# Gated delta rule in a two-block transformer kernel: the convolution's first tap on ScalarE, the decay's column as a bias of the exponential, k times beta in one operation

## The chip, the cores and the metric

The kernel runs on one core of a Trainium2 chip, in one launch. The metric is the device time of that core in microseconds (us), the median of three runs. Matrix products run on TensorE (PE in the profile), elementwise work on VectorE (DVE) and ScalarE (ACT), and GpSimd (POOL) makes the low halves of the weights. SyncE (SP) issues the loads.

## The reference, cut to what matters

512 tokens of width 1024 pass through two layers of a first block and then through a second block. The change is in the second block's gated delta rule: 8 heads, key and value width 128, chunks of 64 tokens.

```python
qkv = jax.nn.silu(_causal_dwconv(jnp.concatenate([qa, ka, va], axis=-1), conv_w[l]))   # 4 taps
...
q = _l2norm(...) * (A_DK ** -0.5); k = _l2norm(...)
beta = jax.nn.sigmoid(beta)
g = -jnp.exp(a_log) * jax.nn.softplus(alpha + dt_bias)
G = jnp.cumsum(g over a chunk)
diff = G[..., :, None] - G[..., None, :]
decay = jnp.where(incl, jnp.exp(jnp.where(incl, diff, 0.0)), 0.0)
L = jnp.where(strict, beta[..., :, None] * kk * decay, 0.0)
rhs = jnp.concatenate([beta[..., None] * v, (beta * jnp.exp(G))[..., None] * k], axis=-1)
sol = triangular_solve(I + L, rhs)
p_intra = einsum("bhncd,bhnjd->bhncj", q, k) * decay
# then a scan over the 8 chunks with q * exp(G), k * exp(g_last - G), exp(g_last)
```

Every projection around it (q, k, v, the output gates, the band attention, the memory attention, the feed-forward) is a dense product with fp32 accuracy.

## The kernel before, in words

**Dense products.** A weight unit is 128x2048 values. ScalarE copies it rounded to its high half (line 2183, `WH<-WR`), GpSimd subtracts to make the low half in pieces of 256 columns (line 3028, `WL<-WR,WH`), and TensorE takes three products for each of 8 slices of the contraction (line 1886: high by high, low by high, high by low). Two buffers hold the halves, so ScalarE's copy of a unit waits until TensorE has finished the unit two before it.

**Order of the work.** A planner (`order`, lines 542 to 1812) writes one list of steps. Each engine's program is that list with the steps that concern the engine, so every engine works in list order and a wait holds all that stands behind it on the same engine. The planner runs a small clock for each engine with estimated costs (the table `ROUGH`, lines 326 to 351; a pair such as `("V", 0.7, 0)` is 0.7 us of VectorE). `weave` (line 504) lets several lanes advance, always the one that is earliest by this clock. The list therefore changes when costs in the table change.

**The delta rule's stage** (`deltanet`, lines 1088 to 1498). Its lanes are the dense projections (`products`), the convolutions, the preparation of each head, the inversion of pairs of heads, the scan over chunks, and the gates. Steps that the change touches:

- `dq1` (line 2775): VectorE multiplies a projected tile of q, k or v by the rows' norm into one of two padded buffers (`pad`). 24 times, 8 heads by 3. A buffer is free again after the last tap, and a projection waits in the planner while both are taken.
- `dq2` (lines 2776 to 2786): the four taps on VectorE. Tap 3 is a `tensor_scalar` (line 2783) with a wait for `dq1` and for the old contents of the destination; taps 2, 1, 0 are multiply-and-add (line 2786). `dq3` (line 2316) is SiLU on ScalarE.
- `gates4` (line 2308): ScalarE copies the turned gate rows to `RC`, four groups of eight columns per block of 128 tokens: G, beta, exp(G), beta's companion for the last decay. Group 0 (G) is read by `p4` alone.
- `p4` (lines 2787 to 2795): G's row, spread by TensorE over a bank, less G's column from `RC` (line 2793), plus a mask into `DT` (line 2795). Then one exponential over 128x512 on ScalarE (line 2331, `pdec`).
- `p4n`, `p4d`, `p12`, `p14` (lines 2796 to 2844): VectorE makes beta over the norm of k, multiplies the decay by it, and multiplies two products by the decay. Step `j1` of the inversion (lines 2853 to 2865) follows `p12`, and each level of the inversion is a round trip between TensorE (lines 2026, 2036, 2045, 2056) and VectorE or ScalarE (lines 2869 to 2877, 2358).
- `p9` (lines 2827 to 2833 and 2340 to 2347): VectorE scales k by a column in four operations of 128x128, then ScalarE scales k by another column in four (`KD`).

Of the kernel before, what the change touches and what calls it, by code (L numbers as in the profile page):

```python
# [94 lines left out]
def memory(nc, ctx):  # L95
# [156 lines left out]
    "nt": ("V:nt",), "dq1": ("V:dq1",), "dq2": ("V:dq2",), "dq3": ("A:dq3",),  # L252
    "p1": ("A:p1q",), "p2": ("A:pks",), "peq": ("V:peq",), "prow": (), "p4": ("V:p4a", "V:p4", "A:pdec"), "p4n": ("V:pkn",), "p4d": ("V:pdn",),
# [22 lines left out]
    "conv_v": "dq1 dq2 padz", "prepare_a": "p1q pks pdec pbv pkd", "prepare_v": "peq pkn psq p4a p4 pdn pbk pum ppt pqd pel",  # L276
# [43 lines left out]
def by_dma(unit):  # L320
# [221 lines left out]
def order(m):  # L542
# [545 lines left out]
    def deltanet(fo, res_toks):  # L1088
# [94 lines left out]
        def convolutions():  # L1183

            for h in range(8):
                for j in range(3):
                    while (h, j) not in pad_of:
                        yield
                    yield from until((read[j], h - 2))
                    pd = pad_of[h, j]  # L1190
                    for k in (3, 2, 1, 0):
                        step("dq2", h, j, k, pad=pd.i, tok=at("dq1", h, j), c_after=cfree["qkv"[j] + str(h % 2)])
                        if k == 0:
                            pd.free(at("dq2", h, j, 0))
                        yield
                    step("dq3", h, j)
                    curved[j].add(h)
                    yield
# [650 lines left out]
def v4(ap):  # L1849
    return ap.rearrange("p (b q) -> p b q", q=P)  # L1850
# [317 lines left out]
def scalar_program(nc, m, o, sems):  # L2168
# [7 lines left out]
    for kind, key, w in o.steps:  # L2176
# [129 lines left out]
        elif kind == "gates4":  # L2306
            ae.wait_ge(*w["tile"].done)
            a.activation(m.RC[:], PB[w["tile"].b][:].rearrange("p (b q r) -> p b q r", b=4, q=4)[:, :, :, 0:8], ACT.Copy).then_inc(sems["rct"], 1)
        elif kind == "gates5":
            ae.wait_ge(*at("rg"))  # L2310
            a.activation(m.RHL[0:32, :], m.R[0:32, :], ACT.Copy)
            a.activation(m.RHL[64:96, :], m.R[64:96, :], ACT.Copy).then_inc(sems["rhi"], 1)
        elif kind == "dq3":
# [15 lines left out]
        elif kind == "p4":  # L2329
            ae.wait_ge(*at("p4", *key))  # L2330
            a.activation(m.DT[:], m.DT[:], ACT.Exp).then_inc(sems["pdec"], 1)
# [122 lines left out]
def vector_program(nc, m, o, sems):  # L2454
# [39 lines left out]
    for kind, key, w in o.steps:  # L2494
# [281 lines left out]
        elif kind == "dq2":  # L2776
# [3 lines left out]
            if k == 3:  # L2780
                ve.wait_ge(*at("dq1", h, j))
                ve.all(w["c_after"])
                v.tensor_scalar(c[:], pad[:, 3:3 + S], tap, None, ALU.mult).then_inc(sems["dq2"], 1)
            else:
                ve.wait_ge(*at("dq2", h, j, k + 1))
                v.scalar_tensor_tensor(c[:], pad[:, k:k + S], tap, c[:], ALU.mult, ALU.add).then_inc(sems["dq2"], 1)
        elif kind == "p4":
            h, = key
            ve.wait_ge(*w["tile"].done)
            ve.wait_ge(*at("rct"))  # L2790
            ve.all(w["after"])
            bank = PB[w["tile"].b]
            v.tensor_tensor(v4(bank[:]), v4(bank[:]), m.RC[:, :, 0, h:h + 1].broadcast_to([P, 4, P]), ALU.subtract).then_inc(sems["p4a"], 1)
            ve.wait_ge(*at("p4a", h))
            v.tensor_tensor(v4(m.DT[:]), v4(bank[:]), over_blocks(m.CON[:, C_INCL:C_INCL + P]), ALU.add).then_inc(sems["p4"], 1)
        elif kind == "p4n":
            h, = key
            x, y = roots_in(PB[w["tile"].b], 4)
            ve.wait_ge(*at("p4", h))
            ve.wait_ge(*at("pks", h))  # L2800
# [26 lines left out]
        elif kind == "p9":  # L2827
# [3 lines left out]
            for i in range(4):  # L2831
                ins = v.tensor_scalar(blk(m.bk[h % 2], i), blk(PB[w["tile"].b], i), m.RC[:, i, 2, h:h + 1], None, ALU.mult)
            ins.then_inc(sems["pbk"], 1)
# [388 lines left out]
```

## Time and profile before

| | |
|---|---|
| median of 3 runs | 2474.83 us |
| lowest and highest run | 2470.92 and 2479.09 us |
| the profiled execution | 2473.95 us |
| its span, first to last instruction | 2472.3 us |
| instructions | 35533 |
| TensorE busy | 98% of the span |
| weight loads busy | 81% |
| VectorE, ScalarE, GpSimd busy | 41%, 38%, 48% |
| mean granted TensorE clock | 0.993 of full speed |

A busy TensorE is not TensorE at its peak, since matmuls overlap and their ends are modelled. A missing fraction of busy time is time in which nothing at all ran on it. The delta rule's stage lies between 1150 and 1560 us of the span.

### The profile page before, as it was taken

What the parts mean: (1) busy time and instruction counts of PE and PEld (TensorE: products, weight loads), DVE (VectorE), ACT (ScalarE), POOL (GpSimd) and SP (SyncE); (2) the same over time, 40 slices, a digit from 0 to 9 for tenths busy, and PEclk for the clock granted to TensorE, in tenths of its full rate; (3) what the DMA queues carried; (4) which work ended last, traced back from release to release, by engine and by line L of the source; (5) the groups of instructions that cost most, each with busy time, mean ns of one, the idle gap of its engine ahead of it and who ended that gap; (6) DMA issues with size and microseconds to landing.
All of it is one profiled execution on the core that took longest, in us unless ns stands there. A gap on an engine that the chain in (4) does not pass through costs nothing.

```text
span 2472.3 us, 35533 instructions
## 1 busy us (share of the span) xinstructions
PE 2425.7 (98%) x14295; PEld 2004.9 (81%) x14295; DVE 1007.0 (41%) x2261; ACT 935.4 (38%) x1435; POOL 1182.7 (48%) x1566
## 2 busy tenths in 40 slices
PE   8999999999999999999999999999999999999998
PEld 6888888888788888888888888877868887888887
DVE  7974211124874211123867774224345333211113
ACT  5553222224563322224544453235553344322221
POOL 5125655654115565655533233443326645655563
PEclk9999999999999999999999999999999999999999
DMA  5532223224632223224211111232213322223222
GB/s 177 139 103 86 102 88 109 99 77 130 164 103 86 103 81 115 85 85 141 94 58 53 53 52 53 81 133 86 69 58 128 116 96 79 96 86 110 103 80 83
DMA packets 42403, 237.17 MB, mean 96 GB/s; under 512 B 4736, under 2 KB 7936, under 8 KB 19712
## 3 DMA queue, kind: packets, MB, share of 16 engines
q1 hardware_dynamic: 39936, 218.13, 25.0%
q0 software_dynamic: 2304, 16.78, 3.3%
q8 instruction: 113, 1.85, 0.3%
q14 instruction: 50, 0.41, 0.1%
HBM read 213.92 MB, written 4.19 MB: 88 GB/s over the span
## 4 chain that ended last, share of the span: by engine, by line
PE 91%; DVE 4%; POOL 2%; issue 1%; ACT 1%; DMA 1%; SPq 0%; DVEq 0%; POOLq 0%; ACTq 0%
PE PB L1886 75%; PE PB L1888 4%; POOL WL L3028 1%; PE PB L1898 1%; PE PB L1923 1%; PE PB L2136 1%; PE PB L2117 1%; DVE cc L2614 1%; PE PB L1970 1%; PE PB L1987 1%; PE PB L2124 1%; DMA WR<-in_w_in 1%; PE PB L2148 1%; PE PB L2164 1%; PE PB L2087 0%
## 5 line engine op out<-in xcount | busy, mean ns | idle before, releaser
L3028 POOL TENSOR_TENSOR WL<-WR,WH 128x256 fp32r<-128x256 f32 (+1 forms) x1444 | 1055.0, 767 | 753.6 <-ACT WH L2183 753.6
L1886 PE MATMUL PB<-HH,WH 128*128 128x512 f32 x1992 | 795.0, 399 | 11.0 <-ACT HH L2198 10.5
L1886 PE MATMUL PB<-HL,WH 128*128 128x512 f32 x1992 | 779.4, 391 | 0.9 <-DVE HL L2506 0.9
L1886 PE MATMUL PB<-HH,WL 128*128 128x512 f32 x1992 | 516.5, 396 | 0.8 <-DMA WL<-WR 0.8
L2183 ACT ACTIVATE WH<-WR 128x2048 fp32r<-128x2048 f32 (+1 forms) x209 | 371.9, 1779 | 245.9 <-PE PB L1886 238.2
L1886 PEld LDWEIGHTS PB<-HH,WH 128*128 128x128 f32 x1992 | 375.8, 189 | 101.2 <-issue 13.7
L1886 PEld LDWEIGHTS PB<-HL,WH 128*128 128x128 f32 x1992 | 375.8, 189 | 76.9 <-issue 1.7
L1886 PEld LDWEIGHTS PB<-HH,WL 128*128 128x128 f32 x1992 | 366.4, 188 | 75.3 <-issue 2.0
L1886 PE MATMUL PB<-BL,WH 128*128 128x512 f32 (+1 forms) x859 | 331.6, 387 | 0.6 <-DVE BL L2515 0.6
L1886 PE MATMUL PB<-BH,WH 128*128 128x512 f32 (+1 forms) x795 | 307.9, 388 | 1.3 <-ACT BH L2218 1.3
L1886 PE MATMUL PB<-BH,WL 128*128 128x512 f32 (+1 forms) x795 | 195.0, 389 | 1.5 <-POOL WL L3028 1.5
L2521 DVE TENSOR_TENSOR X<-X,PB 128x512 f32<-128x512 f32 x79 | 54.3, 687 | 332.3 <-PE PB L1886 332.3
L1886 PEld LDWEIGHTS PB<-BL,WH 128*128 128x128 f32 x859 | 161.5, 188 | 34.0 <-DVE BL L2515 1.4
L1886 PEld LDWEIGHTS PB<-BH,WH 128*128 128x128 f32 x795 | 149.6, 188 | 32.6 <-ACT BH L2218 2.2
L1886 PEld LDWEIGHTS PB<-BH,WL 128*128 128x128 f32 x795 | 148.3, 189 | 33.1 <-POOL WL L3028 3.0
L3043 POOL TENSOR_TENSOR BL<-ff1c,BH 128x512 fp32r<-128x512 f32 x44 | 56.9, 1294 | 168.0 <-ACT BH L2218 168.0
L2218 ACT ACTIVATE BH<-ff1c 128x512 fp32r<-128x512 f32 x44 | 27.8, 632 | 233.4 <-DVE ff1c L2706 233.4
L2471 DVE TENSOR_TENSOR ff1b<-PB,RSTD 128x512 f32<-128x512 f32 x44 | 30.4, 691 | 196.5 <-PE PB L1886 196.5
L2471 DVE TENSOR_TENSOR ff1a<-PB,RSTD 128x512 f32<-128x512 f32 x44 | 30.4, 692 | 176.8 <-PE PB L1886 168.0
L3033 POOL DMA_DIRECT2D WL<-WR x16 | 14.2, 886 | 170.0 <-ACT WL L2186 170.0
L2614 DVE SCALAR_TENSOR_TENSOR cc<-cp,VECS,cc 128x512 f32<-128x512 f32 x120 | 91.4, 809 | 0.0
L2198 ACT ACTIVATE HH<-X,VECS 128x512 fp32r<-128x512 f32 x48 | 33.3, 717 | 110.4 <-DVE X L2521 110.4
(363 smaller groups left out, 2678.4 us busy)
## 6 DMA issues: line engine op xcount, KB each, us to landing
WR<-in_w_gu SPq DMA_DIRECT2D x66, 1024.0 KB, 4.7
WR<-in_w_dn SPq DMA_DIRECT2D x48, 704.0 KB, 4.0
WR<-in_w_in SPq DMA_DIRECT2D x22, 1024.0 KB, 4.8
WL<-WR POOLq DMA_DIRECT2D x16, 1024.0 KB, 6.9
WR<-in_qkv SPq DMA_DIRECT2D x12, 1024.0 KB, 4.7
WR<-in_w_out SPq DMA_DIRECT2D x8, 1024.0 KB, 4.7
WR<-in_qk SPq DMA_DIRECT2D x8, 1024.0 KB, 4.8
WR<-in_gb SPq DMA_DIRECT2D x4, 1024.0 KB, 4.7
```

Source lines behind the costliest of these rows:

```text
L1886: ins = pe.matmul(out[:, 0:n], wt[:, k * cols + j * P:k * cols + (j + 1) * P], x[:, k, t0:t0 + n], start=first, stop=last)
L1888: ins = pe.matmul(out[:, 0:cols], x[:, k, j * P:(j + 1) * P], wt[:, k * cols:(k + 1) * cols], start=first, stop=last)
L1898: ins = pe.matmul(out[:, j0 + b:j0 + b + 1], blk(src, b), ones[:, 0:1], start=(j0 == 0 and b == 0), stop=(b == nb - 1), skip_group_check=True)
L1923: ins = pe.matmul(blk(PB[t.b], i), blk(left, i), blk(right, i), start=True, stop=True)
L2183: a.activation(m.WH[u % 2][:, 0:n], m.WR[u % 2][:, 0:n], ACT.Copy).then_inc(sems["whi"], 1)
L2198: a.activation(m.HH[:, c, :], m.X[:, c, :], ACT.Copy, scale=w["gain"]).then_inc(sems["hh"], 1)
L2218: a.activation(high[:, w["c"], :], w["src"], ACT.Copy).then_inc(sems["bh"], 1)
L2471: v.tensor_tensor(dst, PB[t.b][:, 0:bank_cols], m.RSTD[:], ALU.mult).then_inc(sems[name], 1)
L2521: v.tensor_tensor(m.X[:, c, :], m.X[:, c, :], PB[w["tile"].b][:], ALU.add).then_inc(sems["res"], 1)
L2614: v.scalar_tensor_tensor(m.cc[j][:], m.cp[j][:, k:k + S], vec(f"dw_w{l}", 2 * k + j), m.cc[j][:], ALU.mult, ALU.add).then_inc(sems["tap"], 1)
L3028: g.tensor_tensor(m.WL[u % 2][:, part], m.WR[u % 2][:, part], f32(m.WH[u % 2][:, part]), ALU.subtract).then_inc(sems["wlo"], 1)
L3043: g.tensor_tensor(m.BL[:, w["c"], :], w["src"], f32(high[:, w["c"], :]), ALU.subtract).then_inc(sems["blg"], 1)
```

## The change

What it does:

1. Tap 3 becomes a step of its own, `dq0`, on ScalarE: an activation Copy with the tap's weight as a column scale. Tap 2 on VectorE waits for it. The wait for the destination's old contents moves from VectorE to ScalarE.
2. `RC`'s group 0 is stored negated, in a copy of its own. The subtraction on VectorE (line 2793) goes; the exponential on ScalarE becomes four of 128x128, each with the block's column of minus G as bias.
3. `p9` on VectorE becomes one operation over 128x512 with the column broadcast.
4. The planner's table follows: `dq0` 0.75 on ScalarE, `dq2` 0.78 to 0.8, `p4` from 1.4 and 2.0 to 0.7 and 1.5 (VectorE and ScalarE), `p9` from 1.7 and 1.6 to 0.7 and 1.1.

```diff
-    "p4": [("V", 1.4, 0), ("A", 2.0, 0)],
+    "p4": [("V", 0.7, 0), ("A", 1.5, 0)],
-    "p9": [("V", 1.7, 0), ("A", 1.6, 0)],
+    "p9": [("V", 0.7, 0), ("A", 1.1, 0)],
+    "dq0": [("A", 0.75, 0)],
...
-                    for k in (3, 2, 1, 0):
-                        step("dq2", h, j, k, pad=pd.i, tok=at("dq1", h, j), c_after=cfree["qkv"[j] + str(h % 2)])
+                    step("dq0", h, j, pad=pd.i, tok=at("dq1", h, j), c_after=cfree["qkv"[j] + str(h % 2)])
+                    yield
+                    for k in (2, 1, 0):
+                        step("dq2", h, j, k, pad=pd.i, tok=at("dq0", h, j))
...
-            a.activation(m.RC[:], PB[w["tile"].b][:].rearrange("p (b q r) -> p b q r", b=4, q=4)[:, :, :, 0:8], ACT.Copy).then_inc(sems["rct"], 1)
+            turned = PB[w["tile"].b][:].rearrange("p (b q r) -> p b q r", b=4, q=4)
+            a.activation(m.RC[:, :, 0, :], turned[:, :, 0, 0:8], ACT.Copy, scale=-1.0)
+            a.activation(m.RC[:, :, 1:4, :], turned[:, :, 1:4, 0:8], ACT.Copy).then_inc(sems["rct"], 1)
...
+        elif kind == "dq0":
+            h, j = key
+            ae.wait_ge(*at("dq1", h, j))
+            ae.all(w["c_after"])
+            a.activation(m.cqkv[h % 2][j][:], m.pad[w["pad"]][:, 3:3 + S], ACT.Copy, scale=vec("conv2", 72 + 8 * j + h)).then_inc(sems["dq0"], 1)
...
             ae.wait_ge(*at("p4", *key))
-            a.activation(m.DT[:], m.DT[:], ACT.Exp).then_inc(sems["pdec"], 1)
+            ae.wait_ge(*at("rct"))
+            for i in range(4):
+                ins = a.activation(blk(m.DT, i), blk(m.DT, i), ACT.Exp, bias=m.RC[:, i, 0, h:h + 1])
+            ins.then_inc(sems["pdec"], 1)
...
-            if k == 3:
-                ve.wait_ge(*at("dq1", h, j))
-                ve.all(w["c_after"])
-                v.tensor_scalar(c[:], pad[:, 3:3 + S], tap, None, ALU.mult).then_inc(sems["dq2"], 1)
-            else:
-                ve.wait_ge(*at("dq2", h, j, k + 1))
-                v.scalar_tensor_tensor(c[:], pad[:, k:k + S], tap, c[:], ALU.mult, ALU.add).then_inc(sems["dq2"], 1)
+            ve.wait_ge(*(at("dq0", h, j) if k == 2 else at("dq2", h, j, k + 1)))
+            v.scalar_tensor_tensor(c[:], pad[:, k:k + S], tap, c[:], ALU.mult, ALU.add).then_inc(sems["dq2"], 1)
...
-            v.tensor_tensor(v4(bank[:]), v4(bank[:]), m.RC[:, :, 0, h:h + 1].broadcast_to([P, 4, P]), ALU.subtract).then_inc(sems["p4a"], 1)
...
-            for i in range(4):
-                ins = v.tensor_scalar(blk(m.bk[h % 2], i), blk(PB[w["tile"].b], i), m.RC[:, i, 2, h:h + 1], None, ALU.mult)
-            ins.then_inc(sems["pbk"], 1)
+            v.tensor_tensor(v4(m.bk[h % 2][:]), v4(PB[w["tile"].b][:]), m.RC[:, :, 2, h:h + 1].broadcast_to([P, 4, P]), ALU.mult).then_inc(sems["pbk"], 1)
```

## Rows read from the trace of the kernel before

**Rows 1.** The profile page, busy time of each engine over the span

```profile
PE 2425.7 (98%) x14295; PEld 2004.9 (81%) x14295; DVE 1007.0 (41%) x2261; ACT 935.4 (38%) x1435; POOL 1182.7 (48%) x1566
```

**Rows 2.** The chain that ended last, by engine, whole span

```profile
PE 91%; DVE 4%; POOL 2%; issue 1%; ACT 1%; DMA 1%; SPq 0%; DVEq 0%; POOLq 0%; ACTq 0%
```

**Rows 3.** Busy time by stretch: the delta rule's stage as one stretch

```profile
core 0: us, PE busy (x) PEld busy (x) DVE busy (x) ACT busy (x) POOL busy (x), PEclk, DMA share, GB/s
...
1150.00:1560.00 410.00, 401.06 (x4337) 340.11 (x4336) 270.86 (x669) 186.45 (x347) 160.62 (x200) 0.99 0.20 70
```

**Rows 4.** Waits of TensorE in the stage: us in total, times, longest

```profile
PE PB L2026 <- DVE TC L2865: 2.2, 2, 1.5
...
PE PB L2045 <- DVE TC L2874: 1.1, 1, 1.1
...
PE PB L2056 <- DVE YC L2877: 0.6, 1, 0.6
PE PB L2104 <- ACT UT L2369: 0.5, 1, 0.5
PE PB L2036 <- DVE YC L2869: 0.5, 1, 0.5
PE PB L1886 <- DVE UM L2471: 0.5, 1, 0.5
```

**Rows 5.** Busy time by stretch, columns as in rows 3: five slices of 20 us

```profile
1250.00:1270.00 20.00, 18.15 (x386) 14.41 (x386) 12.01 (x23) 6.63 (x11) 6.29 (x8) 0.91 0.16 56
...
1310.00:1330.00 20.00, 18.47 (x374) 15.35 (x374) 16.93 (x45) 4.37 (x14) 6.64 (x8) 1.00 0.16 55
...
1390.00:1410.00 20.00, 19.47 (x412) 16.43 (x411) 18.02 (x58) 6.51 (x11) 6.03 (x8) 1.00 0.16 55
1410.00:1430.00 20.00, 17.49 (x327) 15.06 (x326) 13.04 (x22) 8.61 (x17) 7.54 (x8) 0.83 0.06 10
...
1470.00:1490.00 20.00, 19.24 (x352) 16.14 (x351) 16.32 (x54) 7.12 (x13) 6.02 (x8) 1.00 0.15 48
```

**Rows 6.** Groups by line, the stage: the tap on VectorE that moves

```profile
L2783 DVE TENSOR_SCALAR cv<-pad,VECS 128x512 f32<-128x512 f32 x8 | 6.0, 744 | 0.1
...
L2783 DVE TENSOR_SCALAR cq<-pad,VECS 128x512 f32<-128x512 f32 x8 | 4.5, 562 | 0.1
...
L2783 DVE TENSOR_SCALAR ck<-pad,VECS 128x512 f32<-128x512 f32 x8 | 4.4, 549 | 0.0
```

**Rows 7.** Groups by line (first row) and the timeline (second): p4's subtraction, p9

```profile
L2793 DVE TENSOR_TENSOR PB<-PB,RC 128x512 f32<-128x512 f32 x8 | 5.5, 690 | 0.0
...
1402.00 1.12 DVE L2832 TENSOR_SCALAR bk<-PB,RC 128x128 f32<-128x128 f32 x4
```

**Rows 8.** ScalarE with a column operand: groups by line and form, and the timeline

```profile
L2198 ACT ACTIVATE HH<-X,VECS 128x512 fp32r<-128x512 f32 x48 | 33.3, 717 | 110.4 <-DVE X L2521 110.4
...
L2394 ACT ACTIVATE bp<-bp,bsm 128x128 f32<-128x128 f32 x16 | 6.2, 389 | 0.2 <-DVE bsm L2947 0.2
...
1403.16 1.14 ACT L2346 ACTIVATE KD<-PB,SMALL 128x128 f32<-128x128 f32 x4 [5.51 <-DVE bk L2832]
```

**Rows 9.** Timeline: one head's exponential, the table load and the SiLU behind it

```profile
1304.80 0.63 ACT L2331 ACTIVATE DT<-DT 128x512 f32<-128x512 f32 x1 [1.64 <-DVE DT L2795]
...
1305.45 1.28 ACT L2316 ACT_TABLE_LOAD   x1
1306.74 0.63 ACT L2316 ACTIVATE cv<-cv 128x512 f32<-128x512 f32 x1
```

**Rows 10.** Timeline: VectorE standing in order ahead of an inversion

```profile
1308.18 0.69 DVE L2471 TENSOR_TENSOR pad<-PB,RSTD 128x512 f32<-128x512 f32 x1 [2.58 <-PE PB L1886]
```

**Rows 11.** Timeline: ScalarE's queue ahead of an inversion's step, and TensorE behind it

```profile
1499.42 1.90 ACT L2183 ACTIVATE WH<-WR 128x2048 fp32r<-128x2048 f32 x1
...
1502.92 0.38 ACT L2358 ACTIVATE YC<-PB 32x256 f32<-32x256 f32 x1
1503.40 0.69 PE L2056 MATMUL PB<-ZC,YC 32*32 32x32 f32 x32 [0.91 <-issue]
```

More of the change, by code:

```diff
@@ L251 @@
     "gates4": ("A:rct",), "gates5": ("A:rhi", "V:rlo"),
-    "nt": ("V:nt",), "dq1": ("V:dq1",), "dq2": ("V:dq2",), "dq3": ("A:dq3",),
-    "p1": ("A:p1q",), "p2": ("A:pks",), "peq": ("V:peq",), "prow": (), "p4": ("V:p4a", "V:p4", "A:pdec"), "p4n": ("V:pkn",), "p4d": ("V:pdn",),
+    "nt": ("V:nt",), "dq1": ("V:dq1",), "dq0": ("A:dq0",), "dq2": ("V:dq2",), "dq3": ("A:dq3",),
+    "p1": ("A:p1q",), "p2": ("A:pks",), "peq": ("V:peq",), "prow": (), "p4": ("V:p4", "A:pdec"), "p4n": ("V:pkn",), "p4d": ("V:pdn",),
     "p5": (), "p6": ("V:psq",), "p6v": ("A:pbv",),
@@ L275 @@
     "ffn_v": "ff1 ff3 ff", "gates_v": "rcol c1 ab dtb udt dcum rg rlast rlo", "gates_a": "beta edt alog ldt reg rdec rct rhi",
-    "conv_v": "dq1 dq2 padz", "prepare_a": "p1q pks pdec pbv pkd", "prepare_v": "peq pkn psq p4a p4 pdn pbk pum ppt pqd pel",
+    "conv_v": "dq1 dq2 padz", "prepare_a": "p1q pks pdec pbv pkd", "prepare_v": "peq pkn psq p4 pdn pbk pum ppt pqd pel",
     "invert_v": "jz0 jz jt jy kv kz", "invert_a": "jd ka iut iwt", "scan_v": "c0 c1u c4", "zgate_v": "za1 zg1 zg",
@@ L2329, in scalar_program @@
         elif kind == "p4":
+            h, = key
             ae.wait_ge(*at("p4", *key))
-            a.activation(m.DT[:], m.DT[:], ACT.Exp).then_inc(sems["pdec"], 1)
+            ae.wait_ge(*at("rct"))
+            for i in range(4):
+                ins = a.activation(blk(m.DT, i), blk(m.DT, i), ACT.Exp, bias=m.RC[:, i, 0, h:h + 1])
+            ins.then_inc(sems["pdec"], 1)
         elif kind == "p6v":
@@ L2789, in vector_program @@
             ve.wait_ge(*w["tile"].done)
-            ve.wait_ge(*at("rct"))
             ve.all(w["after"])
             bank = PB[w["tile"].b]
-            v.tensor_tensor(v4(bank[:]), v4(bank[:]), m.RC[:, :, 0, h:h + 1].broadcast_to([P, 4, P]), ALU.subtract).then_inc(sems["p4a"], 1)
-            ve.wait_ge(*at("p4a", h))
             v.tensor_tensor(v4(m.DT[:]), v4(bank[:]), over_blocks(m.CON[:, C_INCL:C_INCL + P]), ALU.add).then_inc(sems["p4"], 1)
@@ L2799, in vector_program @@
             ve.wait_ge(*at("p4", h))
+            ve.wait_ge(*at("rct"))
             ve.wait_ge(*at("pks", h))
```

6 rows, old and new, of the table ROUGH are left out of this document.

## The prediction

> **What bounds the kernel now.** The page comes first. TensorE is busy for 2425.7 of 2472.3 us, VectorE for 41% and ScalarE for 38% [rows 1], and the chain that ended last runs through TensorE for 91% and through VectorE for 4% [rows 2]. All that any change to the other engines can win is in the 46.6 us in which TensorE does nothing, and in time at a lowered clock. The next view is the busy time by stretch. In the stage of the delta rule, 410 us long, TensorE is busy for 401.1, VectorE for 270.9 (66%), ScalarE for 186.5 (45%) [rows 3]. So 8.9 us of idle TensorE lie in the stage, and the other 37.7 lie where the change has no instruction.
>
> The third view tells what ended TensorE's waits there. Five rows name VectorE: 2.2 + 1.1 + 0.6 + 0.5 + 0.5 = 4.9 us; one names ScalarE, 0.5 us [rows 4]. The slices show where. In the three in which VectorE is busy for over 16 of 20 us, TensorE loses 1.5, 0.5 and 0.8 us, 2.8 together; two others lose 1.9 and 2.5, at a granted clock of 0.91 and 0.83 of full speed [rows 5]. Those means say that 1.8 and 3.4 us of full-speed work were lost to the lower of the two levels (1.2 GHz in place of 2.4), 5.2 us together. Each dip stands in a slice where TensorE had just gone idle.
>
> **The parts of the change, on the engines.** The moved tap takes 4.5 + 4.4 + 6.0 = 14.9 us of VectorE, 24 operations [rows 6]. The subtraction takes 8 x 0.69 = 5.5 [rows 7]. Scaling k by a column takes 1.12 us a head in four operations; the subtraction that goes has the very form of the new one (a bank, a broadcast column, 128x512) at 0.69, so 8 x 0.43 = 3.4 are saved [rows 7]. VectorE gives up 23.8 us: 270.9 becomes 247.1, 60% of the stage.
>
> ScalarE takes 24 copies of 128x512 with a column as scale, at the 0.72 us of such a copy: 17.3 us. The exponential, 0.63 us in one operation [rows 9], becomes four. No row shows four exponentials from SBUF with a column bias behind each other. From below they cost the 1.14 us of four copies with a column [rows 8], from above four single exponentials of 128x128 with a column, 4 x 0.389 = 1.56 [rows 8]. I take 1.2, since one such exponential is only some 0.02 longer than one such copy. That is 8 x 0.57 = 4.6 us more, between 4.1 and 7.4. The second copy of the gate columns is one small operation, under 0.4 us, once. Together 22 us: ScalarE goes from 186.5 to 208.5, 51% of the stage. Neither engine is full before or after. No DMA is added or moved, and GpSimd and the loads keep their steps.
>
> Two chains have to be looked at besides. For a head's decay they were 0.69 + 0.69 + 0.63 = 2.0 us (subtraction, mask, exponential) and become 0.69 + 1.2 = 1.9. For a tap, 0.62 us (14.9 / 24) on VectorE become 0.72 on ScalarE, and two handovers between engines come in; a handover to an idle engine costs little, to a busy one it costs that engine's queue. The added wait for the gate columns at the exponential is met long before, as the columns are made once at the stage's start.
>
> **The sum on TensorE's path.** First, VectorE's earlier freedom. It can be worth nothing, or all 4.9 us that name it. It is not all: ahead of the 1.5 us lost in the slice from 1310, VectorE itself had stood for 2.58 us waiting for a projected tile of TensorE [rows 10], and time saved before such a wait is only a longer wait. I take the losses in the three slices where VectorE is over 16 of 20 us busy, 2.8, and two thirds of them, as 9% less work brings those slices to about 15 to 16.5: **-2.0 us**. Second, the clock. The dip of 3.4 us lies in a slice where VectorE is busy for only 13 of 20 us, so less work there need not fill the hole: **0**, with -5.2 as the end of the range. Third, ScalarE's queue. At 1499 a weight copy of 1.9 us stands ahead of a piece of the inversion; TensorE idles 0.91 us until that piece is there [rows 11]. With the 0.5 us named above, 1.4 us of TensorE hang on a late ScalarE now. 12% more work on it gives 0.2, and the 24 new handovers push steps of this kind back as well: **+0.5**, between 0 and the rival's price below. Fourth, the planner's list. Its table takes p4's part on ScalarE down from 2.0 to 1.5 us, but table load and exponential took 1.28 + 0.63 = 1.9 [rows 9] and will take 1.28 + 1.2 = 2.5. Where the load does not fall into a wait, VectorE's multiplication of the decay stands 1.0 us longer than planned: up to 8 us over 8 heads, if no other work covers it. In the row, the exponential had waited 1.64 us for VectorE [rows 9], long enough for the load to be hidden: **0**. A rewritten list also moves the dense products between the inversion's steps, with either sign and no row to price it; the stage's 8.9 us of idle time bound the gain.
>
> The sum is -2.0 + 0 + 0.5 + 0 = **-1.5 us**. Against the profiled execution (span 2472.3, 1.65 us around it, 2473.95 in all) that is 2472.4. The profiled one lies 0.9 under the median, so the median should be 2474.8 - 1.5 = **2473.3 us**. A measurement of this kernel can tell about 0.3%, 7.4 us, from no change, and this is within it.
>
> The Trainium skill ("ScalarE: Activation LUTs", What ACT_TABLE_LOAD costs) says that a switch of tables costs the load of about 1.28 us and a drain of about 1.38 besides. The trace does not agree: the load begins 0.02 us after the exponential ends, and the SiLU starts 0.01 after the load [rows 9]. By the page a head's exponential would be due 1.4 us later, and the fourth term's end would be 19 us in place of 8.
>
> **Rival A, VectorE's queue was the bound: faster.** A freer VectorE lets every inversion step answer at once, TensorE has no hole, and the clock does not fall. That gives 4.9 + 5.2 = 10.1 us, 2464.7. For it: the slices with the busiest VectorE lose, and the projections wait for the convolution's buffers in the planner. Against it: [rows 10], and that the deepest slice has a VectorE busy only 65%.
>
> **Rival B, the new handover: slower.** The first tap stands in ScalarE's queue behind a weight copy of 1.9 us [rows 11] or a table load and SiLU of 1.9 [rows 9]. VectorE works in order, so while it stands at the second tap the inversion's steps behind it wait too, and TensorE with them. At 51% busy, the mean rest of what ScalarE is doing, half of 0.8 us or so (208.5 us over some 400 operations, the long ones weighing more), is about 0.4 us. Times 24, if all of it reaches TensorE: 9.6 us, 2484.4. It decides the sign beyond noise from 7.4 / 24 = 0.31 us of TensorE's time for each handover. Against it: the planner knows of the handover and lets other lanes go between, and VectorE has 163 us of idle time in the stage. The Trainium skill has a rule that speaks against this move ("ScalarE: Activation LUTs", Rules for kernel authors): multiplications and additions belong on VectorE, not on ScalarE. The rows bear it out for the single operation, 0.62 against 0.72 us, and leave open whether it matters.
>
> **Rival C, nothing.** Both engines' saved and added time falls into their idle time: 2474.8. Copies with a column have no table load of their own in the stage, so no hidden load spoils it.
>
> **The chances.** The forecast has 0.38 and rival C 0.24; both are within 0.3%, 0.62. Rival A, all cases below 2467.4, has 0.25. Rival B, all above 2482.3, has 0.13. The range from 2463.5 to 2483 leaves out about 0.08 below and 0.10 above.
>
> **What the changed profile would show.** VectorE near 247 us in the stage and ScalarE near 208; the new copy at 0.72; the exponential's blocks at 0.3 to 0.4 each, 1.2 for four; one operation of 0.69 for k. TensorE's idle time in the stage between 6 and 9 us. If rival A is right, rows of TensorE waiting for VectorE vanish and the clock's two dips with them. If B is right, waits of VectorE's second tap for ScalarE stand there with several us, and new holes in the inversions. The prediction is wrong if idle time in the stage changes by more than 7 us, or if the later stages, whose instructions are the same, move by as much because of the new list.

## The result, and the profile after

The changed kernel takes 2493.57 us (median of 6 runs, 2489.97 to 2496.61), the kernel before beside it 2477.16 us (6 runs, 2470.92 to 2479.09). The ratio is 1.0071, 95% interval 1.0059 to 1.0084: 16.4 us slower, beyond the 0.3% that a measurement can tell. The forecast was 2473.3 us, its range ended at 2483.0.

The profiled execution took 2493.78 us. Its page, the busy times (beside [rows 1]) and, further down the page, the chain that ended last (beside [rows 2]):

```profile
PE 2431.7 (98%) x14295; PEld 2006.8 (81%) x14295; DVE 984.1 (39%) x2205; ACT 956.1 (38%) x1484; POOL 1175.5 (47%) x1566
...
PE 91%; DVE 4%; POOL 2%; issue 1%; ACT 1%; DMA 1%; SPq 0%; DVEq 0%; POOLq 0%; ACTq 0%
```

The page hardly differs. VectorE has lost 22.9 us of work, ScalarE gained 20.7, as foreseen, and the chain has the same shares. The loss shows only by stretch. After, the delta rule's stage, the later stages, and three slices of the stage (columns as in [rows 3]):

```profile
1150.00:1580.00 430.00, 407.39 (x4336) 342.29 (x4335) 247.31 (x613) 207.05 (x395) 153.70 (x200) 0.97 0.19 67
1580.00:2492.50 912.50, 890.30 (x4607) 731.60 (x4605) 281.02 (x667) 317.56 (x511) 459.43 (x631) 0.99 0.27 94
1220.00:1240.00 20.00, 12.04 (x176) 9.56 (x175) 12.54 (x23) 10.93 (x24) 7.14 (x8) 0.74 0.28 102
1410.00:1430.00 20.00, 15.60 (x426) 12.09 (x425) 11.91 (x34) 4.14 (x11) 3.50 (x5) 0.74 0.16 55
1490.00:1510.00 20.00, 17.84 (x386) 14.34 (x385) 12.46 (x39) 6.28 (x10) 5.57 (x8) 0.83 0.16 55
```

Before, the later stages:

```profile
1560.00:2472.30 912.30, 889.92 (x4605) 731.65 (x4604) 280.66 (x667) 317.43 (x511) 459.68 (x630) 0.99 0.27 94
```

The later stages take 912.5 us against 912.3. All of the loss, 20 us of the profiled span, lies in the delta rule's stage, which does the same number of matmuls (4336, and 4337 in [rows 3]) in 430 us for 410. TensorE is idle in it for 430 - 407.39 = 22.6 us, against 8.9: 13.7 more. The other 6.3 us are busy time, and the granted clock goes with it: 0.97 over the stage for 0.99. The clock and the holes are in the same slices. In the slices from 1220 and 1410 the granted clock is 0.74, and TensorE is idle for 8.0 and 4.4 us.

What ended TensorE's waits in the stage after (columns as in [rows 4]):

```profile
PE PB L2028 <- DVE TC L2869: 8.0, 1, 8.0
PE PB L2038 <- DVE YC L2873: 4.1, 1, 4.1
PE PB L2058 <- issue: 3.9, 2, 2.0
```

The longest wait of before was 1.5 us [rows 4]. Here one wait alone is 8.0, at the first step of the first inversion. The timeline after, around it:

```profile
1222.49 1.64 PE L1888 MATMUL PB<-HH,WL 128*128 128x512 f32 x6
...
1223.43 1.28 ACT L2343 ACT_TABLE_LOAD   x1
...
1224.72 1.28 ACT L2343 ACTIVATE DT<-DT,RC 128x128 f32<-128x128 f32 x4
...
1226.03 0.69 DVE L2819 TENSOR_TENSOR DT<-DT,PB 128x512 f32<-128x512 f32 x1 [1.67 <-ACT DT L2343]
1226.82 0.69 DVE L2843 TENSOR_TENSOR UM<-PB,DT 128x512 f32<-128x512 f32 x1
1227.54 3.06 DVE L2864 SCALAR_TENSOR_TENSOR ZC<-UM,CON 32x256 f32<-32x256 f32 x4
...
1230.64 0.83 DVE L2867 TENSOR_TENSOR ZC<-ZC,CON 128x256 f32<-128x256 f32 x1
1231.50 0.45 DVE L2869 STREAM_TRANSPOSE TC<-ZC 128x256 f32<-128x256 f32 x1
...
1232.09 1.08 PE L2028 MATMUL PB<-TC,UM 32*32 32x32 f32 x64 [7.96 <-DVE TC L2869]
```

From 1224.13 (1222.49 + 1.64) to 1232.09 ScalarE and VectorE make the inversion's first operand (the decay's exponential, two products, then the operand itself), as they must in either kernel. The point is TensorE's column: behind six dense matmuls (L1888) the very next thing in its program is L2028. Nothing is listed between. Before, the same place is covered. The timeline before, the dense products that go on behind the same six and the inversion's first step:

```profile
1222.52 1.63 PE L1886 MATMUL PB<-HH,WL 128*128 128x512 f32 x6
1223.99 0.39 PE L1886 MATMUL PB<-HH,WH 128*128 128x512 f32 x1
...
1235.63 0.75 PE L2026 MATMUL PB<-TC,UM 32*32 32x32 f32 x64
```

The same 14 us as one stretch (busy time by stretch), before:

```profile
1222.00:1236.00 14.00, 14.00 (x112) 11.65 (x113) 11.55 (x24) 6.33 (x13) 6.00 (x8) 1.00 0.37 125
```

After:

```profile
1222.00:1236.00 14.00, 6.04 (x145) 4.55 (x143) 10.13 (x18) 8.20 (x17) 7.14 (x8) 0.72 0.07 28
```

VectorE is no busier in this stretch than before (10.13 us for 11.55). TensorE has no dense product to do.

Two readings of this fit so far. Either the new instructions make the chain later than the planner thinks (rival B, or the underpriced `p4`), or the list itself is worse, and any instructions would run badly in it. The planner can be asked as well. It prints no time of the chip, but its own clock says when it believes TensorE to be free. Run for the two kernels, it gives for the end of the stage, and for what TensorE stands idle in the plan:

```
          TensorE's clock at the stage's end   idle TensorE in the stage's plan
before    1661.4                               22.4
after     1685.5                               46.5, of it 8.48 ahead of the first inversion's first step
```

The hole of 8 us thus stands in the plan, and could have been read there before anything ran. The planner's clock has no unit that can be trusted (a plan's 24.1 us are 16.4 on the chip), but the hole is in the plan.

### The profile page after: what moved, and what is told of

Same layout as the page of the kernel before. It is cut to its first block, busy times and chain, and to the rows that moved or that the text cites. A ratio compares the mean times of both kernels' runs of the same rounds, so it can differ in the third digit from the quotient of the medians.

```text
span 2492.5 us, 35533 instructions
## 1 busy us (share of the span) xinstructions
PE 2431.7 (98%) x14295; PEld 2006.8 (81%) x14295; DVE 984.1 (39%) x2205; ACT 956.1 (38%) x1484; POOL 1175.5 (47%) x1566
## 4 chain that ended last, share of the span: by engine, by line
PE 91%; DVE 4%; POOL 2%; issue 1%; ACT 1%; DMA 1%; SPq 0%; DVEq 0%; POOLq 0%; ACTq 0%
PE PB L1888 75%; PE PB L1890 4%; POOL WL L3032 1%; PE PB L1925 1%; PE PB L1900 1%; PE PB L2138 1%; PE PB L2119 1%; DVE cc L2627 1%; PE PB L1972 1%; PE PB L2126 1%; PE PB L1989 1%; DMA WR<-in_w_in 1%; PE PB L2150 1%; PE PB L2166 1%; PE PB L2089 1%
## 5 line engine op out<-in xcount | busy, mean ns | idle before, releaser
L1888 PE MATMUL PB<-HH,WH 128*128 128x512 f32 x1992 | 797.4, 400 | 10.3 <-ACT HH L2200 9.8
L1888 PE MATMUL PB<-HL,WH 128*128 128x512 f32 x1992 | 781.2, 392 | 2.0 <-DVE HL L2519 2.0
L1888 PE MATMUL PB<-HH,WL 128*128 128x512 f32 x1992 | 517.0, 396 | 0.9 <-DMA WL<-WR 0.9
L1888 PEld LDWEIGHTS PB<-HH,WH 128*128 128x128 f32 x1992 | 376.6, 189 | 100.9 <-issue 13.7
L1888 PEld LDWEIGHTS PB<-HL,WH 128*128 128x128 f32 x1992 | 376.8, 189 | 78.1 <-DVE HL L2519 2.5
L1888 PEld LDWEIGHTS PB<-HH,WL 128*128 128x128 f32 x1992 | 365.2, 188 | 74.8 <-issue 2.0
L1888 PE MATMUL PB<-BL,WH 128*128 128x512 f32 (+1 forms) x859 | 331.4, 387 | 0.6 <-DVE BL L2528 0.6
L1888 PE MATMUL PB<-BH,WH 128*128 128x512 f32 (+1 forms) x795 | 307.9, 388 | 1.3 <-ACT BH L2220 1.3
L1888 PE MATMUL PB<-BH,WL 128*128 128x512 f32 (+1 forms) x795 | 195.1, 389 | 1.5 <-POOL WL L3032 1.5
L1888 PEld LDWEIGHTS PB<-BL,WH 128*128 128x128 f32 x859 | 161.5, 188 | 34.0 <-DVE BL L2528 1.4
L1888 PEld LDWEIGHTS PB<-BH,WH 128*128 128x128 f32 x795 | 149.5, 188 | 32.6 <-ACT BH L2220 2.2
L1888 PEld LDWEIGHTS PB<-BH,WL 128*128 128x128 f32 x795 | 148.5, 189 | 33.2 <-POOL WL L3032 3.0
```

Source lines behind the costliest of these rows:

```text
L1888: ins = pe.matmul(out[:, 0:n], wt[:, k * cols + j * P:k * cols + (j + 1) * P], x[:, k, t0:t0 + n], start=first, stop=last)
```

## The experiments

### The list against the instructions

Two kernels separate them. `new_ops_old_list` has all of after's instructions, while the planner counts them by the costs of before and counts the tap as VectorE's, so that the list of steps is the one of before, step for step. The entries of the table that change:

```diff
-    "dq0": [("A", 0.75, 0)], "dq2": [("V", 0.8, 0)],
+    "dq0": [("V", 0.78, 0)], "dq2": [("V", 0.78, 0)],
-    "p4": [("V", 0.7, 0), ("A", 1.5, 0)],
+    "p4": [("V", 1.4, 0), ("A", 2.0, 0)],
-    "p9": [("V", 0.7, 0), ("A", 1.1, 0)],
+    "p9": [("V", 1.7, 0), ("A", 1.6, 0)],
```

> All of the change's instructions, but the planner's table keeps the old costs and counts the first tap as 0.78 us of VectorE, so every engine works through the list of before. Theory L (the loss comes from the new list: the planner has both padded buffers held, lists no dense product ahead of an inversion, and TensorE runs dry there): the loss of 16.4 us is gone, the time is 2470 to 2479 us, and TensorE's wait of 8 us near 1232 us is not there. Rival E (the loss comes from the handover to ScalarE's queue, whatever the list): 2488 to 2498 us, with VectorE's second tap waiting for ScalarE and holes in the inversions.

`old_ops_new_list` is the converse: before's instructions (tap on VectorE, subtraction, one exponential, k in four), in the list of after. The tap is a step `dq0` of its own for that, planned as ScalarE's and executed by VectorE. Against before, the entries of the table that change and the step:

```diff
+    "dq0": [("A", 0.75, 0)], "dq2": [("V", 0.8, 0)],
...
+    "p4": [("V", 0.7, 0), ("A", 1.5, 0)],
...
+    "p9": [("V", 0.7, 0), ("A", 1.1, 0)],
...
+        elif kind == "dq0":
+            h, j = key
+            ve.wait_ge(*at("dq1", h, j))
+            ve.all(w["c_after"])
+            v.tensor_scalar(m.cqkv[h % 2][j][:], m.pad[w["pad"]][:, 3:3 + S], vec("conv2", 72 + 8 * j + h), None, ALU.mult).then_inc(sems["dq0"], 1)
```

> The instructions of before (first tap on VectorE, subtraction on VectorE, one exponential, four operations for k), in the list that the changed table gives. Theory L: slow like the changed kernel or slower, 2490 to 2500 us, with TensorE waiting about 8 us before the first inversion. Rival E: as before, 2472 to 2480 us.

Measured: the new instructions in the old list 2479.35 us beside 2477.92, ratio 1.0005 (0.9995 to 1.0015, 11 runs). The old instructions in the new list 2495.07, ratio 1.0069 (1.0056 to 1.0081, 5 runs). After itself is 1.0071. So the instructions, all of them together, are worth nothing that can be measured in either list, and the list is worth the whole loss. The longest waits of TensorE in `old_ops_new_list`:

```profile
PE PB L2028 <- DVE TC L2867: 7.4, 3, 6.7
PE PB L2038 <- DVE YC L2871: 4.2, 1, 4.2
```

Its timeline at the same place:

```profile
1223.50 1.64 PE L1888 MATMUL PB<-HH,WL 128*128 128x512 f32 x6
1231.84 1.08 PE L2028 MATMUL PB<-TC,UM 32*32 32x32 f32 x64 [6.70 <-DVE TC L2867]
```

The same hole at the same place, 6.70 us long for 7.96, without one changed instruction. The new instructions lengthen this one by 1.3 us and the total by nothing.

The stage of `new_ops_old_list` by stretch:

```profile
1150.00:1560.00 410.00, 399.76 (x4325) 338.93 (x4324) 249.79 (x613) 206.73 (x395) 155.22 (x195) 0.98 0.20 70
```

Its timeline at the same place, TensorE:

```profile
1223.56 1.64 PE L1888 MATMUL PB<-HH,WL 128*128 128x512 f32 x6
1225.04 0.39 PE L1888 MATMUL PB<-HH,WH 128*128 128x512 f32 x1
```

Dense products follow the six again, and TensorE idles for 10.2 us of the stage's 410, for 8.9 before. The five waits that the prediction's first term was built on ([rows 4], 4.9 us, all naming VectorE) are still there, each with the total that it had, although VectorE now has 249.8 us of work in the stage in place of 270.9. Waits of TensorE in `new_ops_old_list`:

```profile
PE PB L2028 <- DVE TC L2869: 2.2, 3, 1.5
...
PE PB L2047 <- DVE TC L2878: 1.1, 1, 1.1
...
PE PB L2058 <- DVE YC L2881: 0.6, 1, 0.6
...
PE PB L2038 <- DVE YC L2873: 0.5, 1, 0.5
PE PB L1888 <- DVE UM L2484: 0.5, 1, 0.5
```

This run decides on rival B too. Its mechanism was VectorE standing at the second tap. Waits of VectorE in `new_ops_old_list`, then in after:

```profile
DVE cv L2794 <- ACT cv L2321: 9.7, 2, 7.1
DVE cq L2794 <- ACT cq L2321: 5.8, 3, 3.2
```

```profile
DVE cv L2794 <- ACT cv L2321: 3.2, 3, 1.3
DVE cq L2794 <- ACT cq L2321: 1.0, 1, 1.0
```

VectorE stands 15.5 us at the handover where the kernel loses nothing that can be measured, and 4.2 us where it loses 16. So the handover does not make the loss. What it costs by itself no run shows apart from what the freed VectorE gives: the two together come to +1.2 us, between -1.2 and +3.7 by the interval of the ratio.

### Which part makes the list worse

`tap_only` has the moved tap and its costs, the decay and `p9` as before. `decay_only` has the decay's bias and k in one operation with their costs, the tap on VectorE.

The table of `tap_only`, against after (its instructions for the decay and for k are before's too):

```diff
-    "p4": [("V", 0.7, 0), ("A", 1.5, 0)],
+    "p4": [("V", 1.4, 0), ("A", 2.0, 0)],
...
-    "p9": [("V", 0.7, 0), ("A", 1.1, 0)],
+    "p9": [("V", 1.7, 0), ("A", 1.6, 0)],
```

The lane in `decay_only`, against after (the tap's cost and instruction are before's again too):

```diff
-                    step("dq0", h, j, pad=pd.i, tok=at("dq1", h, j), c_after=cfree["qkv"[j] + str(h % 2)])
-                    yield
-                    for k in (2, 1, 0):
-                        step("dq2", h, j, k, pad=pd.i, tok=at("dq0", h, j))
+                    for k in (3, 2, 1, 0):
+                        step("dq2", h, j, k, pad=pd.i, tok=at("dq1", h, j), c_after=cfree["qkv"[j] + str(h % 2)])
```

> Only the first tap moves to ScalarE, with its costs in the table; the decay and k times beta stay as before. The planner's own clock has the delta rule's stage end 46.9 us later than for the kernel before (24.1 us later for the whole change). Theory L, with the tap's handover as its cause: clearly slower than before, 2495 to 2530 us, slower than the whole change. Rival E: about the whole change's loss, 2485 to 2497 us. A third reading (the decay's and k's cheaper costs spoil the list, not the tap): as before, 2472 to 2480 us.

> The decay's column as a bias and k times beta in one operation, with their costs in the table; the first tap stays on VectorE. The planner's own clock has the stage end 3.1 us earlier than before. Theory L: 2468 to 2477 us, as before or up to 6 us faster. Rival E: as before too, 2472 to 2480 us, since the tap's handover is not there. The third reading (these costs spoil the list): 2488 to 2498 us.

Measured: `tap_only` 2514.75 us, ratio 1.0142 (1.0128 to 1.0155, 4 runs). `decay_only` 2477.44, ratio 1.0001 (0.9989 to 1.0013, 11 runs). The tap alone loses twice what the whole change loses, and the decay's part alone is worth nothing. The parts do not add (1.42% and 0.01% for a whole of 0.71%). On top of the moved tap, the lower costs of `p4` and `p9` give half of the loss back (1.0142 to 1.0071); alone they give nothing. `tap_only`'s waits of TensorE, of the kind seen after:

```profile
PE PB L2028 <- DVE TC L2867: 14.8, 3, 7.3
PE PB L2038 <- DVE YC L2871: 4.5, 2, 3.0
```

### Why the tap does it: the convolutions' lane

In the planner the convolutions are one lane. For each of 24 tiles it issues `dq1`, the taps and the SiLU, and each step moves the lane's own time to where that step can start. With the tap on ScalarE the lane waits twice a tile for ScalarE's place in the plan, once for the tap and once for the SiLU, and the next tile's taps queue behind both. The dates of the planner for the first head that matters say so (end of `dq1`, of the first tap, of the last tap, of the SiLU), and the last SiLU of the stage:

```
                 before                             after
head 1, q        1209.6 1225.3 1233.0 1234.1        1209.7 1226.6 1234.4 1237.8
head 1, k        1228.3 1238.9 1242.4 1243.5        1227.5 1241.7 1244.6 1245.7
head 1, v        1238.1 1244.3 1246.6 1249.0        1235.1 1250.7 1260.0 1261.1
last SiLU        1515.4                             1542.3
```

While both padded buffers are held, the lane of the dense projections waits in the planner. The plan of after says that this is so at the hole. In the 8.48 us without TensorE the two buffers hold head 1's v and head 2's q. The projection behind them is computed and stands at the wait for a free buffer, and the last tap that frees one (head 1's v, 1260.0 in the plan, 1246.6 before) is listed behind the inversion's first step. Of TensorE's idle time in the stage's plan, the part in which the dense lane stands at that wait is 12.5 of 22.4 us before, 29.6 of 46.5 after, and 46.4 of 69.4 in `tap_only`.

Two kernels try the cause. The diffs leave out unchanged lines (marked by dots) and the name of the new lane in the call of `weave`. `tap_own_lane` is after with the same instructions and costs, but the tap is issued from a lane of its own, so that a tile's tap can be placed while the tile before it is still in its taps:

```diff
-                    while (h, j) not in pad_of:
+                    while (h, j) not in begun:
...
-                    yield from until((read[j], h - 2))
...
-                    step("dq0", h, j, pad=pd.i, tok=at("dq1", h, j), c_after=cfree["qkv"[j] + str(h % 2)])
-                    yield
...
+        def first_taps():
...
+            for h in range(8):
+                for j in range(3):
+                    while (h, j) not in pad_of:
+                        yield
+                    yield from until((read[j], h - 2))
+                    step("dq0", h, j, pad=pad_of[h, j].i, tok=at("dq1", h, j), c_after=cfree["qkv"[j] + str(h % 2)])
+                    begun.add((h, j))
+                    yield
```

> The changed kernel, but in the planner the first tap is a lane of its own instead of the first step of the convolutions' lane: it may be listed as soon as its tile is in a padded buffer, while the tile before it still waits for its SiLU. Instructions and table are those of the changed kernel. Theory S (the loss comes from the convolutions' lane being serial: with the tap on ScalarE each tile waits twice for ScalarE's place in the plan, 24 tiles come later, and TensorE has nothing to list between the inversions' steps): 2470 to 2482 us; the planner's own clock has the stage end at 1659.4, 1685.5 for the changed kernel and 1661.4 for the one before. Theory B (the cause is the number of padded buffers alone, which stay held longer whatever the lanes): 2486 to 2498 us.

`three_pads` leaves the lanes alone and gives the convolutions a third padded buffer:

```diff
-    m.pad = (pad0, pad1)
+    pad2, = run(spot["bv1"] + 2048, spot["z0"], ("pad2", [P, 3 + S]))
+    m.pad = (pad0, pad1, pad2)
...
-        pads = Ring([Room(0), Room(1)], clock)
+        pads = Ring([Room(0), Room(1), Room(2)], clock)
```

> The changed kernel with a third padded buffer for the convolutions. Theory B (TensorE runs dry because both padded buffers are held): 2472 to 2482 us. Theory S (the serial lane sets the pace; a buffer more only moves the holes): the hole of 8 us ahead of the first inversion goes, others take its place, 2488 to 2500 us (the planner's own clock: 1685.7, as for the changed kernel).

Measured: `tap_own_lane` 2471.32 us beside 2476.8, ratio 0.9978 (0.9969 to 0.9987, 12 runs). The loss is gone and a little is gained. `three_pads` 2499.99, ratio 1.0092 (1.0076 to 1.0108, 4 runs): no cure. The stage of `tap_own_lane` by stretch:

```profile
1150.00:1560.00 410.00, 404.51 (x4338) 342.19 (x4337) 247.24 (x614) 208.14 (x396) 156.66 (x199) 0.98 0.20 71
```

VectorE's and ScalarE's work is that of after to within 1.1 us. TensorE's idle time is 5.5 us in 410, for 22.6 in 430.

Longest waits in `three_pads`:

```profile
PE PB L2029 <- DVE TC L2870: 9.2, 3, 3.3
PE PB L2081 <- DVE SS L2915: 6.6, 2, 3.6
PE PB L2039 <- DVE YC L2874: 6.0, 2, 3.0
```

The hole of 8 us is broken up (no wait is over 3.6 us), but others take its place, at other inversions and in the scan. So the place of the tap in a serial lane is shown to be the cause: moving that one step to another lane, with every instruction and cost kept, takes the loss away. A third buffer did not help, and the planner's idle TensorE stayed at 46.7 (46.5 after, 20.5 with the own lane). The plan says why. In eight of the ten longest holes of `three_pads` all three buffers are held, and the dense lane stands at its wait for one in 24.2 us of the 46.7, against 5.3 with the tap's own lane. Full buffers are how the dense products are kept out. That they are full comes from the slow lane that empties them, and one more is soon full too.

### The other ScalarE step in the lane

If a serial lane is the trouble, the SiLU in it is a second wait for ScalarE, in before too. Three kernels move `dq3` to a lane of its own: `after_silu_lane`, `decay_silu_lane` (from `decay_only`) and `before_silu_lane`.

```diff
-                    step("dq3", h, j)
+                    tapped.add((h, j))
...
+        def silus():
...
+            for h in range(8):
+                for j in range(3):
+                    while (h, j) not in tapped:
+                        yield
+                    step("dq3", h, j, tok=at("dq2", h, j, 0))
```

> The changed kernel, but the SiLU behind the taps gets a lane of its own in the planner, so that the convolutions' lane waits for ScalarE's place once per tile, as in the kernel before, though now for the first tap. Theory S: 2466 to 2480 us (planner's own clock 1657.7). If the tap's own wait is what costs, whatever else is in the lane: 2486 to 2498 us.

> The first tap stays on VectorE; the decay's bias and k times beta in one operation are in; the SiLU gets a lane of its own, so that the convolutions' lane never waits for ScalarE's place. Planner's own clock: 1648.5, 12.9 us before that of the kernel before. Theory S: faster than both kernels, 2462 to 2472 us. If the planner's clock says nothing about small gains: 2472 to 2480 us.

> The kernel before with nothing but the SiLU in a lane of its own in the planner. It tells whether the gain of the run with the SiLU's own lane belongs to the lane or to the lane together with the change. Planner's own clock: 1668.0 for the end of the stage, 1661.4 for the kernel before. If the lane alone gains: 2464 to 2472 us. If it gains only with the change's cheaper VectorE work (as the planner's clock has it): 2476 to 2488 us.

Measured: `after_silu_lane` 2467.56 us, ratio 0.9955 (0.9940 to 0.9971, 6 runs). `decay_silu_lane` 2471.06, ratio 0.9975 (0.9962 to 0.9988, 12 runs). `before_silu_lane` 2482.97 beside 2477.11, ratio 1.0028 (1.0017 to 1.0040, 6 runs). The same edit wins 1.2% on after (1.0071 to 0.9955), 0.3% on `decay_only`, and loses 0.3% on before. The first of the three says more on the cause. The tap's step is still in the lane there, and the loss is gone all the same. So it takes both waits for ScalarE in one lane, the tap's and the SiLU's, and taking out either is enough. The rule "a lane of its own is better" is wrong as a rule, though the last two differences are no larger than the 0.3% that a measurement can tell; what the lane is worth depends on the costs in the table beside it.

One question was whether the new instructions are at last worth something in this better list. `old_ops_silu_list` has before's instructions in the list of `after_silu_lane`, made as `old_ops_new_list` was:

> The list of the changed kernel with the SiLU's own lane, with the instructions of the kernel before. Beside that kernel (2467.6 us) it prices the change's instructions in a good list. If they are worth nothing in themselves, as in the list of before: 2466 to 2471 us. If VectorE's 24 us less work counts there: 2472 to 2482 us.

Measured: 2464.4 us, ratio 0.9955 (0.9942 to 0.9969, 5 runs), the same ratio as `after_silu_lane`, each taken against the kernel before that ran beside it. Its stage:

```profile
1150.00:1550.00 400.00, 395.36 (x4316) 334.54 (x4315) 270.04 (x669) 186.40 (x346) 154.02 (x192) 1.00 0.21 72
```

VectorE has its old 270 us and TensorE idles for 4.6 us of 400. A VectorE busy for two thirds of the stage was no limit, or none that the change's instructions relieve.

The last one, `silu_lane_costs`, puts into `after_silu_lane`'s table what the profile measured for `p4` (load and four exponentials, 1.28 + 1.28) and `p9`, and a little less for a tap:

```diff
-    "dq2": [("V", 0.8, 0)],  "p4": [("V", 0.7, 0), ("A", 1.5, 0)],  "p9": [("V", 0.7, 0), ("A", 1.1, 0)],
+    "dq2": [("V", 0.76, 0)], "p4": [("V", 0.7, 0), ("A", 2.5, 0)],  "p9": [("V", 0.7, 0), ("A", 1.2, 0)],
```

> The changed kernel with the SiLU's own lane and the table brought nearer to the measured durations (decay on ScalarE 2.5 in place of 1.5, k's scaling 1.2 in place of 1.1, a tap 0.76 in place of 0.80). Planner's own clock: 1654.0, 3.7 before that of the run with the lane alone. If differences of a few us in the planner's clock carry over: 2461 to 2467 us. If they are lost in what it doesn't model: 2464 to 2474 us.

Measured: 2463.63 us, ratio 0.9945 (0.9932 to 0.9959, 5 runs), the fastest of all, 1.3% below after; its interval overlaps that of `after_silu_lane`. Its stage by stretch:

```profile
1150.00:1550.00 400.00, 397.58 (x4338) 338.26 (x4337) 247.50 (x614) 208.03 (x397) 155.25 (x200) 1.00 0.20 72
```

Its longest wait of TensorE in the stage:

```profile
PE PB L2099 <- DVE UU L2912: 0.7, 1, 0.7
```

2.4 us of idle time are left in 400, at a granted clock of 1.00. Little is left to win in this stage by order alone.

### The lists side by side

| kernel | planner's clock against before's 1661.4 | ratio measured |
|---|---|---|
| `tap_only` | +46.9 | 1.0142 |
| `three_pads` | +24.3 | 1.0092 |
| after | +24.1 | 1.0071 |
| `old_ops_new_list` | +24.1 | 1.0069 |
| `before_silu_lane` | +6.6 | 1.0028 |
| `new_ops_old_list` | 0 | 1.0005 |
| `tap_own_lane` | -2.0 | 0.9978 |
| `decay_only` | -3.1 | 1.0001 |
| `after_silu_lane` | -3.7 | 0.9955 |
| `old_ops_silu_list` | -3.7 | 0.9955 |
| `silu_lane_costs` | -7.5 | 0.9945 |
| `decay_silu_lane` | -12.9 | 0.9975 |

Every step up in the planner's clock was a loss, with 0.7 to 1.05 times its size in us. Among the lists at or below before's, the clock does not rank: -12.9 gave 6.2 us, -3.7 gave 11.1.

## Why the prediction was wrong

**What held.** The costs of the parts did. Groups by line in the stage after, for the exponential, its table load, the tap and k:

```profile
L2343 ACT ACT_TABLE_LOAD x8 | 10.3, 1283 | 0.1
L2343 ACT ACTIVATE DT<-DT,RC 128x128 f32<-128x128 f32 x32 | 10.3, 390 | 4.5 <-DVE DT L2800 4.5
L2321 ACT ACTIVATE cv<-pad,VECS 128x512 f32<-128x512 f32 x8 | 5.8, 728 | 0.6 <-DVE pad L2484 0.6
...
L2837 DVE TENSOR_TENSOR bk<-PB,RC 128x512 f32<-128x512 f32 x8 | 5.4, 671 | 0.0
```

The tap takes 0.71 to 0.73 us (0.72 forecast), k in one operation 0.67 (0.69), four exponentials 10.3 / 8 = 1.28 with gaps (1.2, inside its bounds of 1.14 and 1.56). VectorE has 247.3 us in the stage (247.1), ScalarE 207.1 (208.5). The later stages did not move. The Trainium skill's drain of some 1.38 us besides a table load ("ScalarE: Activation LUTs", What ACT_TABLE_LOAD costs) does not show here either: load at 1223.43, 1.28 long, exponential at 1224.72.

**First term, VectorE's freedom: -2.0.** Not borne out. The change's instructions, with over 20 us less on VectorE, are worth nothing in three lists: before's (1.0005), after's (1.0071 against 1.0069), the SiLU lane's (0.9955 against 0.9955). The interval of the first, 0.9995 to 1.0015, leaves at most 1.2 us of gain for this term and the third together, for which the prediction had 1.5. The five waits that it counted stand unchanged in `new_ops_old_list`, 4.9 us. The two thirds of 2.8 us were a choice on rows that named VectorE as the releaser. How full VectorE is does not set those waits, and the list does. In `old_ops_silu_list`, where VectorE has all of its old work, no wait of TensorE for one of the inversions' steps on VectorE is left; what still names VectorE there is 1.4 us at other places. Rival A's mechanism falls with it. Its sentence "the projections wait for the convolution's buffers in the planner" pointed at the right part of the program and took it for a reason to gain.

**Second term, the clock: 0.** Wrong in a direction that had no bound. Only the two old dips were priced, as something to win back. Three slices after lie at 0.74, 0.74 and 0.83, and 6.3 us of the loss are busy time. The clock goes with the holes in the main: 0.95 to 0.97 over the stage in the profiles with 20 us of idle time or more, 0.99 or 1.00 in the four with the SiLU's own lane and the change's costs. It is no strict order, as `decay_only` has 0.96 at 11 us of idle time.

**Third term, ScalarE's queue: +0.5.** Not refuted, and not measured by itself. In the list of before VectorE stands at the handovers for 15.5 us, and the instructions as a whole cost 0.05%, not to be told from nothing. With no sign of a gain to be set against it, this term cannot be much over 3.7 us, the upper end of that interval.

**Fourth term, the planner's list: 0. This is the step that failed.** The prediction saw that the list would be rewritten, "with either sign and no row to price it", bounded the gain by 8.9 us of idle time and gave the loss no bound at all; it then took 0 and gave this branch no chance of its own. It measured +17 us (1.0069), the whole result. The moved tap made the convolutions' lane wait twice a tile for ScalarE, the padded buffers stayed full, and the dense products that had covered the first inversion were listed elsewhere. Two things were there to be read. The change puts a new `yield` and a ScalarE step into the middle of a serial lane with 24 passes, ahead of an engine that the table has as busier. And the planner's rule stands in the code: a step's cost on another engine moves the lane's time, and the lane holds buffers that the dense products need. A third was to be had: the planner's clock, run for the two tables, puts the stage's end 24.1 us later. From the code alone the sign would still have been uncertain, as `before_silu_lane` shows, where less in the lane is a loss. As for the size, lists of the change's very instructions came out here between 0.9945 and 1.0092, 36 us. A term with that spread must widen the range on both sides.

**Rival B, 2484.4, slower.** It had the right sign, over half of the size (9.6 of 16.4 us, which is luck), and the right element (the tap's handover), but the wrong mechanism. It happens in the plan, not in the queue at run time: the waits that it named are 3.2 and 1.0 us after. So its test, "waits of VectorE's second tap stand there with several us", came out weak while the kernel lost 16 us. The other test, that idle time in the stage changes by more than 7 us, gave the verdict: it changed by 13.7.

**The underpriced `p4`.** Planned with 1.5 us of ScalarE, it takes 2.56. At the hole it is visible: VectorE waited 1.67 us for the exponential, and the hole is 7.96 with the new instructions and 6.70 with the old. Over the kernel it costs nothing measurable (1.0071 against 1.0069), and the costs nearer to the measured ones in the table of `silu_lane_costs`, together with its smaller cost of a tap, gave 0.1%, within the intervals.

What stays open is how well the plan foretells single holes. Its two longest in the stage after, 8.48 and 4.73 us, meet waits of 8.0 and 4.1 on the chip, but `decay_silu_lane`, the best list by its clock, is beaten on the chip by three others of the table.

## What to carry to other kernels

Where engines run a list written by a planner, an edit has two parts: the instructions, and the list that the new costs make. Run them apart, new instructions in the old list and old instructions in the new list, before a gain or a loss is put down to an operation; here the second was everything. A step moved to another engine inside a serial lane should be given a lane of its own or be tried with and without, and as the spread between lists of the same instructions can be larger than any such edit is worth (here 1.5%), it belongs into the range from the start.

## What the runs showed of the hardware beyond that

**Small operations of VectorE beside GpSimd.** The inversion's first four operations, 32 partitions by 256, take 1.71 us in an inversion where GpSimd is idle and 3.57 in one where it makes weight halves. Timeline of before, VectorE in two inversions and GpSimd in the first (in the second it had nothing):

```profile
1310.22 3.57 DVE L2860 SCALAR_TENSOR_TENSOR ZC<-UM,CON 32x256 f32<-32x256 f32 x4
...
1471.67 1.71 DVE L2860 SCALAR_TENSOR_TENSOR ZC<-UM,CON 32x256 f32<-32x256 f32 x4
...
1310.16 5.94 POOL L3028 TENSOR_TENSOR WL<-WR,WH 128x256 fp32r<-128x256 f32 x7 [7.37 <-ACT WH L2183]
```

A single one goes from 0.42 to 0.95 us, about the length of a piece on GpSimd (5.94 / 7 = 0.85). The Trainium skill ("SBUF — State Buffer", SBUF: two separate sides) says that a VectorE operation with two inputs in SBUF and a GpSimd operation that reads SBUF take turns, each for a whole instruction. The rows agree with it. In after's hole this group runs beside GpSimd and takes 3.06 us. By this reading, for which no run took GpSimd away, 1.4 of those 8 us are GpSimd's, an estimate from the two groups.

**The clock after a hole.** In the last part of the hole of 7.96 us and behind it the granted clock is at its lower level (1.2 GHz). Here 5 us of after as one stretch, 2.1 of them in the hole:

```profile
1230.00:1235.00 5.00, 2.91 (x68) 2.13 (x68) 4.27 (x7) 0.54 (x2) 5.00 (x6) 0.50 0.02 3
```

The timeline after, two dense matmuls of those 5 us:

```profile
1233.70 0.63 PE L1888 MATMUL PB<-HL,WH 128*128 128x512 f32 x1
1234.12 0.63 PE L1888 MATMUL PB<-HH,WH 128*128 128x512 f32 x1
```

They start 0.42 us apart. In the covered stretch of before they start 0.23 apart (1223.99 and, next, 1224.22). This hole is paid for a second time after its end.
